# Hybrid attention and mixture-of-experts trunk: the input projection on x without the norm's factor, its loop written out, and empty scatters held by GpSimd

## What is computed

```python
def rms_norm(x, g):
    y = x32 * lax.rsqrt(jnp.mean(x32 * x32, axis=-1, keepdims=True) + RMS_EPS)
    return (y * g.astype(jnp.float32)).astype(x.dtype)
...
for l in range(DEPTH):
    h = rms_norm(x, norm1_gain[l])
    z = h @ w_in[l]
    q, k, v, u = jnp.split(z, [ATT_WIDTH, 2 * ATT_WIDTH, 3 * ATT_WIDTH], axis=-1)
    q = rms_norm(q.reshape(B, S, N_HEADS, HEAD_DIM), q_norm_gain[l]).astype(jnp.float32)
    k = rms_norm(k.reshape(B, S, N_HEADS, HEAD_DIM), k_norm_gain[l]).astype(jnp.float32)
    q = apply_partial_rope(q, cos, sin) * scale
    k = apply_partial_rope(k, cos, sin)
    v = v.reshape(B, S, N_HEADS, HEAD_DIM).astype(jnp.float32)
    att = dilated_attention(q, k, v).reshape(B, S, ATT_WIDTH).astype(x.dtype)
    pool = pool_mixer(u, w_pool[l], pool_scale[l])
    x = x + jnp.concatenate([att, pool], axis=-1) @ w_out[l]
    x = x + hier_moe(rms_norm(x, norm2_gain[l]), w_group[l], b_group[l], w_router[l], b_router[l],
                     w_gate[l], w_up[l], w_down[l])
return x
```

## Time and profile before

| | |
|---|---|
| runs | 1663.27 us median of 3 (1661.2 to 1667.27) |
| profiled execution | 1666.6 us, span 1664.8 us, mean granted TensorE clock 0.936 |
| busy share | PE 86%, PE weight loads 69%, DVE 60%, ACT 40%, POOL 21% |
| chain that ended last | PE 60%, DMA 14%, DVE 10%, issue 9%, ACT 4% |
| DMA | 204.46 MB, mean 123 GB/s |

### The profile page before, as it was taken

How to read it: one execution, slowest core, us unless ns; L and a number is a source line. 1 busy time by engine, 2 the same in 40 slices (tenths; PEclk the granted TensorE clock), 3 DMA queues, 4 the chain that set the end, 5 groups by cost and what they waited for, 6 DMA issues and landing times.

```text
span 1664.8 us, 24259 instructions
## 1 busy us (share of the span) xinstructions
PE 1427.9 (86%) x7323; PEld 1142.5 (69%) x7324; DVE 997.0 (60%) x1919; ACT 666.1 (40%) x1028; POOL 348.0 (21%) x204
## 2 busy tenths in 40 slices
PE   5999978998995699999299999699989938999981
PEld 4887868887784466666178788688968826666650
DVE  6777666664446666666467866756534475556560
ACT  4232145673211355555332313556611124555450
POOL 1000059002000123233510000950100011223324
PEclk9999988999998799999699999989999959999995
DMA  8100020000129599984770001100001665989937
GB/s 313 31 1 0 0 102 2 1 2 13 51 80 371 168 285 298 341 223 101 162 239 0 1 0 65 38 1 1 2 14 75 232 223 163 274 258 311 294 50 127
DMA packets 115873, 204.46 MB, mean 123 GB/s; under 512 B 9816, under 2 KB 76576, under 8 KB 115776
## 3 DMA queue, kind: packets, MB, share of 16 engines
q1 hardware_dynamic: 90976, 130.77, 22.9%
q0 software_dynamic: 19136, 53.67, 14.6%
q10 hardware_dynamic: 5664, 18.88, 2.9%
HBM read 169.72 MB, written 49.28 MB: 132 GB/s over the span
## 4 chain that ended last, share of the span: by engine, by line
PE 60%; DMA 14%; DVE 10%; issue 9%; ACT 4%; DVEq 2%; POOL 1%; ACTq 1%; SPq 0%; POOLq 0%; PEld 0%; PEldq 0%
PE ps L1501 18%; DMA out_x<-x_res,arena 11%; PE ps L1634 9%; PE ps L1481 9%; PE ps L1715 7%; PE ps L1587 7%; PE ps L1730 4%; PE ps L1561 2%; DMA big<-in_w_in 2%; PE ps L1563 1%; PE ps L1651 1%; DVE arena L1262 1%; DVEq L1372 1%; DVE xgT_lo L1376 1%; PE ps L1621 1%
## 5 line engine op out<-in xcount | busy, mean ns | idle before, releaser
L1367 DVE TENSOR_TENSOR gu_lo<-big,gu_hi 128x2048 fp32r<-128x2048 f32 x96 | 218.6, 2291 | 166.4 <-ACT gu_hi L892 133.0
L1481 PE MATMUL ps<-cst,arena 128*128 128x128 f32 x1226 | 183.2, 283 | 75.1 <-DVE arena L1019 32.9
L1481 PEld LDWEIGHTS ps<-cst,arena 128*128 128x128 f32 x1226 | 148.3, 145 | 124.7 <-DVE arena L1019 34.9
L1501 PE MATMUL ps<-w_in_hi,hT_hi 128*128 128x512 f32 x512 | 204.9, 400 | 12.8 <-DVE hT_lo L1037 10.0
L1501 PE MATMUL ps<-w_in_hi,hT_lo 128*128 128x512 f32 x512 | 201.3, 393 | 0.0
L1501 PE MATMUL ps<-w_in_lo,hT_hi 128*128 128x512 f32 x512 | 201.0, 393 | 0.0
L671 POOL DMA_INDIRECT x_res<-token_rows,row_tok x62 | 91.7, 1479 | 516.0 <-issue 308.7
L892 ACT ACTIVATE gu_hi<-big 128x2048 fp32r (+1 forms) x96 | 181.4, 1916 | 35.3 <-PE ps L1715 35.0
L1715 PE MATMUL ps<-gu_hi,xgT_hi 128*128 128x512 f32 x360 | 150.1, 417 | 23.6 <-DVE xgT_lo L1376 23.6
L1730 PE MATMUL ps<-big,arena 128*128 x360 | 163.8, 598 | 4.7 <-issue 4.7
L1156 DVE CUSTOM_DVE_ANT_0 arena<-ps,cst 128x128 f32<-128x128 f32 (+7 forms) x128 | 96.8, 756 | 102.7 <-PE ps L1563 102.2
(11 more groups left out here) (182 smaller groups left out, 2306.2 us busy)
## 6 DMA issues: line engine op xcount, KB each, us to landing
big<-in_w_gate SPq DMA_DIRECT2D x32, 1024.0 KB, 9.2
big<-in_w_up SPq DMA_DIRECT2D x32, 1024.0 KB, 13.9
big<-in_w_down SPq DMA_DIRECT2D x32, 1024.0 KB, 14.0
big<-in_w_in SPq DMA_DIRECT2D x14, 1024.0 KB, 10.1
big<-in_w_out SPq DMA_DIRECT2D x4, 2048.0 KB, 10.4
token_rows<-arena ACTq DMA_DIRECT2D x16, 512.0 KB, 3.2
out_x<-x_res ACTq DMA_DIRECT2D x16, 512.0 KB, 4.0
x_res<-out_x SPq DMA_DIRECT2D x8, 512.0 KB, 5.9
```

Of the source, the lines that this page charges most:

```text
L1367: ve.tensor_tensor(out=gu_lo[i], in0=raw, in1=gu_hi[i].bitcast(f32), op=ALU.subtract)\
L1481: ins = te.transpose(ps[:, bank + i // 4, (i % 4) * P:(i % 4 + 1) * P], src, ident)
L1501: ins = te.matmul(ps[:, 2 + 2 * par_ + i, :], a[par_][:, k, :], b[:, k, :], start=k == 0 and n == 0, stop=k == K - 1 and n == 2)
```

## The change

It does the following.

- PE transposes x itself (`xr`), not xs; xs and norm_x_again go. r is stored once per token tile in `st[:, 128 + t]`. It multiplies where the product leaves PSUM: as ACT's scale in the square of q and k and in the copies of v and u, and in DVE's last small step of norm_qk (on 8 columns).
- At the start and at the turn of the layers DVE does the gain step before norm_x. At the turn ACT does both pieces of in_high of the first column block before square_x, and DVE both pieces of in_low before gain1.
- `steps` is no longer used in the input projection: the loops over 8 tiles are written out on PE, ACT and DVE (the outer loop over the layers stays).
- A new semaphore may_add: ACT raises it by one with each real block, and by 15 once (behind spare_may and in_high in layer 0, behind the last real block in layer 1). GpSimd waits for it in add_rows, ahead of y0_ready and y1_ready. ACT no longer waits for spare_may in the unused blocks.
- In an unused block PE gives xtm_done before maybe_down instead of after it.

```diff
@@ -675,6 +678,7 @@
+                    pool.wait_ge(may_add, j + 1)
                     pool.wait_ge(y0_ready, upto(l, BLOCKS, j + 1))
@@ -691,6 +695,9 @@
                     add_rows(j)
+                pool.wait_ge(may_clear, upto(l, 1, 1))
+                pool.sem_inc(s_passed, 1)
+                pool.sem_clear(may_add)
             pool.wait_ge(s_add, upto_added(DEPTH, 0))
...
@@ -711,9 +718,8 @@
                 a_.wait_ge(x_ready, upto(l, T, t + 1))
-                if not first(t):
-                    a_.wait_ge(xs_ready, upto(l, 2 * T, t))
-                    a_.wait_ge(xt_done, upto(l, 2 * T, t))
+                if t >= 2:
+                    a_.wait_ge(r_ready, upto(l, T, t - 1))
                 ch.link(sc.activation(xs, xr[:, t, :], ACT.Square, accum_out=st[:, par_:par_ + 1]))
@@ -770,7 +776,9 @@
                     a_.wait_ge(z_done, upto(l, 4 * T, 2 * n + 1))
-                    sc.activation(sqz, ps[:, 2 + 2 * par_, :].rearrange("p (h c) -> p h c", c=HD), ACT.Square)\
+                    a_.wait_ge(r_ready, upto(l, T, t + 1))
+                    sc.activation(sqz, ps[:, 2 + 2 * par_, :].rearrange("p (h c) -> p h c", c=HD), ACT.Square,
+                                  scale=st[:, 128 + t:129 + t])\
                         .then_inc(sqz_done, 1)
...
@@ -790,14 +798,16 @@
                     if h == 0:
-                        sc.activation(v[:, t, :], src, ACT.Copy).then_inc(v_copied, 1)
+                        sc.activation(v[:, t, :], src, ACT.Copy, scale=st[:, 128 + t:129 + t]).then_inc(v_copied, 1)
                     else:
-                        sc.activation(u_nat, src.rearrange("p (g c) -> p g c", g=NG), ACT.Copy).then_inc(u_copied, 1)
+                        sc.activation(u_nat, src.rearrange("p (g c) -> p g c", g=NG), ACT.Copy,
+                                      scale=st[:, 128 + t:129 + t]).then_inc(u_copied, 1)
                     if h == 0 and last(t, T):
                 for h in range(2):
-                    steps(a_, T, lambda t, par_, m: in_act(t, par_, h), ch)
+                    for t in range(T):
+                        in_act(t, t % 2, h)
                     if h == 0:
@@ -906,6 +916,7 @@
                     sc.activation(y[slot][:, 512:1024], ps[:, 5, :], ACT.Copy).then_inc(y1_ready, 1)
+                    a_.sem_inc(may_add, 1)
@@ -939,8 +950,10 @@
                         a_.sem_inc(s_passed, 1)
+                        with a_.If(l > 0):
+                            a_.sem_inc(may_add, SPARE)
+                            a_.sem_inc(may_clear, 1)
                     with a_.Else():
-                        a_.wait_ge(spare_may, upto(l, 1, 1))
                         a_.sem_inc(y1_ready, 1)
@@ -977,10 +990,12 @@
                     sc.activation(st[:, 158:159], eps, ACT.Sqrt)
-                    in_high(l + 1, 0, [0])
+                    first_gain(l + 1)
+                    in_high(l + 1, 0)
+                    a_.wait_ge(spare_may, upto(l, 1, 1))
+                    a_.sem_inc(may_add, SPARE)
+                    a_.sem_inc(may_clear, 1)
                     square_x(l + 1, 0, 0)
-                    first_gain(l + 1)
-                    in_high(l + 1, 0, [1])
                     in_high(l + 1, 1)
...
@@ -1013,16 +1028,8 @@
                 dve.wait_ge(sd1, upto(l, T, t + 1))
-                r = st[:, 4 + par_:5 + par_]
-                rsqrt(st[:, par_:par_ + 1], st[:, 2 + par_:3 + par_], r, st[:, 6:7], 1.0 / D)
-                ve.tensor_copy(st[:, ds(128 + t, 1)], r)
-                ve.tensor_scalar(xs, xr[:, t, :], r, None, ALU.mult).then_inc(xs_ready, 1)
-
-            def norm_x_again(l, t):
-                dve.wait_ge(xt_done, upto(l, 2 * T, T + t))
-                dve.sem_inc(s_passed, 1)
-                ch.link(ve.tensor_copy(st[:, 7:8], st[:, ds(128 + t, 1)]))
-                ve.tensor_scalar(xs, xr[:, t, :], st[:, 7:8], None, ALU.mult).then_inc(xs_ready, 1)
+                rsqrt(st[:, par_:par_ + 1], st[:, 2 + par_:3 + par_], st[:, 128 + t:129 + t], st[:, 6:7], 1.0 / D)
+                dve.sem_inc(r_ready, 1)
@@ -1050,20 +1057,14 @@
                 n = h * T + t
-                if h == 0:
-                    if not last(t, T):
-                        norm_x(l, t + 1, 1 - par_)
-                    else:
-                        norm_x_again(l, 0)
-                elif not (first(t) or last(t, T)):
-                    norm_x_again(l, t + 1)
+                if h == 0 and not last(t, T):
+                    norm_x(l, t + 1, 1 - par_)
                 if h == 0 or not last(t, T):
                 if h == 0 and last(t, T):
-                    norm_x_again(l, 1)
                     in_low(l, 3)
@@ -1080,7 +1081,8 @@
                 ch.link(ve.tensor_scalar(tmp, tmp, -0.5 * scale, 1.5 * scale, ALU.mult, ALU.add))
-                ch.link(ve.tensor_tensor(out=r, in0=tmp, in1=r, op=ALU.mult))
+                ch.link(ve.scalar_tensor_tensor(out=r, in0=tmp, scalar=st[:, 128 + t:129 + t], in1=r,
+                                                op0=ALU.mult, op1=ALU.mult))
                 z = zn[par_]
@@ -1103,11 +1105,10 @@
+            dve.wait_ge(gain_in, upto(0, 1, 1))
+            gain1(0, 0, 0)
             norm_x(0, 0, 0)
-            dve.wait_ge(gain_in, upto(0, 1, 1))
-            in_low(0, 0, [0])
-            gain1(0, 0, 0)
-            in_low(0, 0, [1])
+            in_low(0, 0)
             in_low(0, 1)
@@ -1118,8 +1119,8 @@
                 ch.restart()
-                steps(dve, T, lambda t, par_, m: in_dve(l, t, par_, 0), ch, begun=True)
-                steps(dve, T, lambda t, par_, m: in_dve(l, t, par_, 1), ch)
+                for n in range(1, 2 * T):
+                    in_dve(l, n % T, n % 2, n // T)
@@ -1452,11 +1453,10 @@
                 with dve.If(l < DEPTH - 1):
-                    in_low(l + 1, 0, [0])
-                    norm_x(l + 1, 0, 0)
-                    in_low(l + 1, 0, [1])
+                    in_low(l + 1, 0)
                     dve.wait_ge(gain_in, upto(l + 1, 1, 1))
                     gain1(l + 1, 0, 0)
+                    norm_x(l + 1, 0, 0)
                     in_low(l + 1, 1)
@@ -1487,8 +1487,9 @@
                 def xt(n):
-                    pe.wait_ge(xs_ready, upto(l, 2 * T, n + 1))
-                    transposes(0, cols(xs, K)).then_inc(xt_done, 1)
+                    if n < T:
+                        pe.wait_ge(x_ready, upto(l, T, n + 1))
+                    transposes(0, cols(xr[:, n % T, :], K)).then_inc(xt_done, 1)
@@ -1514,6 +1515,7 @@
+                pe.wait_ge(xgT_ready, upto(l, BLOCKS, 0))
                 xt(0)
@@ -1540,7 +1542,8 @@
                 for h in range(2):
-                    steps(pe, T, lambda t, par_, m: in_pe(t, par_, h))
+                    for t in range(T):
+                        in_pe(t, t % 2, h)
                 turn(1, T - 1, (T - 1) % 2)
@@ -1772,11 +1775,12 @@
                     with pe.Else():
+                        if not last(t, BLOCKS):
+                            pe.wait_ge(xtm_done, upto(l, BLOCKS, t + 1))
+                            pe.sem_inc(xtm_done, 1)
                         maybe_down(t - 1)
                         pe.sem_inc(gu_done, 1)
-                        if not last(t, BLOCKS):
-                            pe.sem_inc(xtm_done, 1)
                         pe.sem_inc(a_t_done, 1)
```

More of the change, by code:

```diff
@@ L395, in trunk @@
         SURE = (2 * SEQ // P - 1) // RING
+        SPARE = BLOCKS - 2 * SEQ // P
         def before(slot, m):
@@ L575, in _ @@
                     load_in((l + 1) % DEPTH, 0, 0)
-            sp.sem_inc(spare_may, 1)
         @block.gpsimd
```

10 lines of the change are left out of this document (6 added, 4 removed).

## The result

The changed kernel took 1646.83 us in the median of 4 runs (1643.95 to 1649.96), the kernel before beside it 1665.27 (4 runs, 1661.2 to 1670.48): ratio 0.9878, 95% interval 0.9842 to 0.9914. The forecast was 1645.2. The total is right; its largest term is not.

What follows compares the result with a forecast made beforehand. TensorE was taken to bound the input projection, and TensorE alternating with a scatter cycle the MoE. Gains of 3.8 + 1.3 + 11.7 + 1.3 = 18.1 us took the median 1663.3 to 1645.2 us, range 1639 to 1657.

Steps and rivals of the forecast that it cites:

- Start: Start of the kernel: transposes need only x, first matmul at 15.9 instead of 17.97; gain 3.8 us, bounds 2.1 and 4.
- Change of weights: Between the input projection's halves: without norm_x_again the lower weights come earlier; 0.65 us a layer, 1.3 us in all.
- Tail: Last real scatter of layer 1: earlier increment lets it start 0.84 us after y; gain 1.3 us, bounds 0 and 2.
- Seam: Between the layers: early walk, held scatters and unscaled x start layer 1 sooner; gain 11.7 us, bounds 6.7 and 12.5.
- ACT's walk: Seam: ACT walks the empty branches at once from 802.4, ending at 810.1 instead of 818.07; 6.8 us needing no data.
- First matmul at 821.7: Seam: layer 1's first matmul starts at 821.7, after transposes to 817.5 and gain steps (3.4), instead of 831.37.
- First empty scatter at 816.4: Seam: first empty scatter comes after ACT's in_high, at 816.4 instead of 812.11; until then x and weights are alone.
- the weights at 822: Seam: layer 1's second weights, freed from sharing with empty scatters, land at 822, bounds 819 and 827.4.
- rival (a): Seam set by transfers, weights as before or tile 2 late: seam gives 6.7, total 1650.2 (1651.7 with both); chance 0.23.
- The rest: Other increments, waits, factors and the written-out loop: together 0, bounds a gain of 1 and a loss of 2.
- (b): Seam does not move, as ACT's walk or SP's steps set it: gain 6.4, total 1656.9; chance 0.09.
- (c): MoE: GpSimd's new wait enters the scatter cycle, 45 real blocks pay 37.8 us, total 1683; chance 0.05.

Runs made afterwards that it cites:

- b_shift: Kernel before with 96 more semaphore increments ahead of ScalarE's outer loop, shifting only the place of its later instructions; 1677.52 us in one run.
- b_again: Kernel before, unedited, run once more for a second trace; 1668.06 us in one run.
- u_inc: Changed kernel with xtm_done of an unused block given after the last down projection again; 1652.01 us in one run.
- n_only: Changed kernel without ACT's early walk, GpSimd's may_add wait and TensorE's earlier increment; keeps unscaled x, new step order, written-out loop; 1651.73 us, ratio 0.9896.
- a_again: Changed kernel, unedited, measured again; 1650.23 us against 1664.24 for the kernel before, ratio 0.9904.
- b_act: Kernel before with the input projection's loop written out on ScalarE alone; 1667.87 us, ratio 1.0022.
- u_hold: Changed kernel with ACT waiting for spare_may in unused blocks again and GpSimd without may_add; 1651.49 us, ratio 0.9908.
- h_real: Changed kernel with ACT releasing the empty scatters only when its first weight conversion has finished; 1646.55 us, ratio 0.9859 to the kernel before.
- b_written: Kernel before with only the input projection's token-tile loop written out on PE, ACT and DVE; 1660.9 us, ratio 0.9993.
- p_hold: p_ahead with the empty scatters released only behind the conversion of the second weight block; 1645.16 us, ratio 0.9866 to the kernel before.
- p_ahead: Changed kernel with TensorE doing layer 1's first transposes before the turn of its outer loop; 1644.44 us, ratio 0.9846 to the kernel before.
- p_real: p_ahead together with h_real's wait; 1646.78 us, ratio 0.9881 to the kernel before.

## Why the prediction was right, and where it was not

**Start: right.** Mean of A over the four traces with the scaled x (without b_shift) 103.18, over the nine with the unscaled x 99.28: 3.9 us, forecast 3.8; 3.5 us without b_again, whose granted clock was low there. In the first pair of traces alone it is 2.15, mostly because x tile 1 landed at 24.1, 1.4 us later. One reading of the prediction has no row of the clock behind it: that half of the first 24 matmuls ran at 1.2 GHz. The granted clock reads 1.00 from 17.97 to 22 us, though the matmuls follow each other every 0.43 us there and every 0.23 us from 23.2 on.

**Change of weights: right.** B went from 131.20 to 130.41, 0.8 us a layer, forecast 0.65.

**Tail: right in size, under a condition.** 1.3 us where TensorE's last down projection ends just before y, and u_inc and n_only beside a_again show it to be the increment's. b_act shows the condition that the prediction left out. In the trace of after TensorE ended 1.48 us before y's move, so there most of the 1.3 us would have been had without the increment.

**Seam: the term of 11.7 was mis-sized.** By C it is 4.7 us: 113.16 as the mean of before and b_again, less 108.42, the mean of the five kernels from after to u_inc. Its steps in turn:

- *ACT's walk*: right, its table load moved from 14.8 to 6.4 us behind the scatter (forecast 6.9). It is worth nothing: n_only, without it, has the same second square (31.63 and 31.65) and the same third gain step as a_again. ACT waits for the second weight block either way.
- *First matmul at 821.7, 18.5 behind the scatter*: measured 23.5 to 27.1. The failing step is "the transposes (1.97) end at 817.5". I took TensorE's 25.68 us of idle time, put down to DVE, for a time in which TensorE was ready. It was walking through its own unused blocks until 813.7 and turning its outer loop until 820.9. Both were to be read in the trace of before, by the source lines of TensorE's queue instead of its timeline. With 820.9 the first matmul would have been put at 826.5. The traces of after and u_hold are a further 3 us late; in after, one branch within the walk takes 2.78 us (source line L1775), in u_hold one of 3.16, in a_again none over 0.66:

```profile
L1775 PEldq COMPARE_BRANCH  x10: 173/208/2782, 785.5 to 806.4; - x10
```

- *First empty scatter at 816.4, and so the weights at 822*: measured 8.7 us behind the last real one instead of 13.2, and ACT's conversion of the second block at 23.5 to 26.0, before 24.1. The failing step is that the increment would come "after ACT's in_high". It stands behind in_high in the program but is not an engine operation: ACT's queue gave it at 803.71, before the two activations of together 3.69 us had even begun (803.91), and the scatter started at 804.71. With a wait for the activation's end (h_real) the scatter comes at 12.7 and the weights follow. The mechanism was right, and it was not in force.
- *What then gave 4.7 us*: the unscaled x, with the order of steps that it allows. Take n_only, which beside that has only the written-out loop (against b_written, which has that loop too, C is 4.65 us shorter). From the second square to the second gain step it needs 4.1 us instead of 5.9, since the transposes run beside the norm instead of behind it and the scaling. From there to the eighth gain step it needs 72.2 instead of 76.1, since TensorE goes on without a gap. In the kernel before it stood still once more, for the scaled x of tile 2 (timeline of PE, before):

```profile
854.08 1.09 PE L1481 MATMUL ps<-cst,arena 128*128 128x128 f32 x8 [2.40 <-DVE arena L1019]
```

  The second square itself comes 0.5 us later. 1.8 + 3.9 - 0.5 = 5.2 us, which is 113.2 less 108.0. (b_written shows 0.5 us of it as well; that may be the loop's.)

This is rival (a), weights as before, and less than its 6.7.

**The rest: wrong by 1.9 us to the good.** D is 0.9 us shorter in each layer, from the written-out loop.

**Rivals.** (a) holds for the seam. (b) does not: the seam moved. (c) is refuted: from y to the DMA are 0.85 us in after (chain of waits: y's move starts at 1528.63 and takes 0.61, the DMA starts at 1530.09), 0.84 before.

**So why was the total right?** In part by luck. Read from the intervals, the parts make 3.9 + 1.6 + 4.7 + 1.9 + 1.3 = 13.4 us, a ratio of 0.992. That lies inside a_again's interval (0.9881 to 0.9927), but outside that of the first comparison (0.9842 to 0.9914). The forecast's 18.1 was met by four runs that came out some us short. The measured medians' distance is 14 us in the one and 18.4 in the other. One part isn't in the sum: in layer 0, for which the prediction took the earlier increment as worth nothing, the scatter started 0.86, 2.09, 0.85, 1.83 and 2.12 us behind y in the five traces with the scaled x, 2.09 in n_only, and 0.85 to 0.95 wherever the increment comes first or in u_inc. What else may lie between the 13.4 and these is in the MoE: layer 1, from first to last real scatter, took 229.9 to 237.3 us in the five traces with the scaled x (mean 233.2) and 229.4 to 235.3 in the nine others (231.6), layer 0 220.5 to 226.5 (223.2) and 219.8 to 224.7 (221.4). With such a spread that is not shown to be a difference. It stays open.

## What to carry over

A long idle row with a releaser says what came last, not that the engine was ready before. Ahead of pulling its work forward, read the engine's own queue by source line: the walk through unused branches and the turn of an outer loop (6.0 to 7.6 us here with full DMA engines) are a floor under every gain, and behind TensorE's turn stands DVE's. A semaphore increment written behind an activation doesn't wait for it; whoever means "when this is done" has to attach it to the instruction or wait for its semaphore first. And an early release that frees one engine is worth nothing if the next thing it needs, here the second weight block, lands when it did.

## What the runs showed of the hardware

The turn of the outer loop costs TensorE 5.98 to 7.58 us in thirteen traces, with the DMA engines full during it (share 0.97 to 1.07), and 4.26 in p_hold, where the first empty scatter started only as it ended (source line above; share 0.17). ACT's and DVE's turns are the "issue" of 5.04 and 2.92 us in before (the latter in the earlier trace rows). DVE's goes the same way: 3.23 us in after, share 0.31 from 838.9 to 842.0, but 5.08, 5.63 and 5.70 in h_real, p_ahead and p_real, shares 0.70, 0.87 and 1.05. The Trainium skill, "Runtime: NRT & Kernel Launch", section "Instruction fetch mechanics", says that a taken branch to a target outside the small window of instructions held forces a fetch of it by DMA before the engine goes on. The rows agree with that: in after the instruction queue moved 4 packets with 0.07 MB from 801 to 822 us, 2 of them during the turn, and the turn was shortest where the other queues had least to move. That it is the fetch was not tested by itself.

The granted clock of TensorE in the attention differs between executions of the same work at the same place. Windows of before, then of after (stretch, its length, busy time and count of each engine, PEclk, DMA share, GB/s):

```profile
294.00:300.00 6.00, 5.90 (x36) 5.90 (x37) 2.38 (x7) 3.49 (x8) 0.00 (x0) 0.67 0.00 0
300.00:306.00 6.00, 6.00 (x42) 5.87 (x40) 1.69 (x5) 2.54 (x6) 0.00 (x0) 0.76 0.00 0
```
```profile
294.00:300.00 6.00, 6.00 (x53) 5.87 (x53) 1.99 (x6) 3.29 (x10) 0.00 (x0) 1.00 0.00 0
```

At 0.67 TensorE was part of the time at the lower of its two levels (1.2 GHz); from 298 to 302 it was 0.50. It had stood idle just before, at a place where it does so in after too, without a fall of the clock (timelines of PE, before and after):

```profile
294.10 0.44 PE L1481 MATMUL ps<-cst,arena 128*128 128x128 f32 x2 [2.06 <-DVE arena L1166]
```
```profile
291.14 0.44 PE L1481 MATMUL ps<-cst,arena 128*128 128x128 f32 x2 [1.74 <-DVE arena L1167]
```

Layer 0's attention took 155.46 us in before, 152.19 in after. Stretches at 0.50 lie in every attention of either kernel; where they fall differs from run to run, and with it the attention's time (152.1 to 157.0 us over all traces). In a_again, layer 1's took 156.97 us, after's 152.16: TensorE had stood 3.31 us to 1098.14, and the granted clock was 0.50 from 1102 to 1107, where after had 1.00. That is 3 to 5 us between two runs of one kernel.
